# Attention over two head slots at a time in a one-layer decoder kernel

## What is computed

```
ada = silu(c) @ W_ada + b_ada              # shift1, scale1, gate1, shift2, scale2, gate2
u   = LN(x) * (1 + scale1) + shift1
xp, q, k, v, g_p, g_a = split(u @ w_in)    # 512 | 768 | 768 | 768 | 1024 | 1024
for group, (window, dilation) in enumerate(((128, 1), (512, 4), (2048, 16))):
    s = q_h @ k_h.T * 64 ** -0.5           # 4 heads of 64 a group; causal, windowed, dilated mask
    p = exp(s - max(s)); den = sum(p); o = p @ v_h / den; lse = max(s) + log(den)
attn   = sum over groups of softmax(lse over groups) * o      # one result a head slot
merged = sigmoid(g_p) * (pool_y @ w_pool_out) + sigmoid(g_a) * (attn @ w_attn_out)
x   = LN(alpha * x + (1 + gate1) * (merged @ w_o))
u2  = LN(x) * (1 + scale2) + shift2
x   = LN(alpha * x + (1 + gate2) * moe(u2))                   # top 4 of 32 clamped SwiGLU experts
```

## Time and profile before

| | us |
|---|---|
| median of 3 executions | 1194.89 (1194.87 to 1195.72) |
| the profiled execution, its own time | 1195.32 |
| its span in the profile | 1193.5 |
| PE busy | 1141.9 (96%) |
| DVE busy | 341.6 (29%) |
| ACT busy | 130.9 (11%) |
| DMA over the span | 461.84 MB, 387 GB/s |

### The profile page before, as it was taken

One profiled execution on the slowest core, in us unless ns is written; L12 is line 12 of the kernel. 1 busy time (PEld: TensorE's weight loads), 2 busy tenths in 40 slices (PEclk: granted clock), 3 DMA queues, 4 the chain that ended last, 5 costly groups with the idle time before them and its releaser, 6 DMA issues.

```text
span 1193.5 us, 13616 instructions
## 1 busy us (share of the span) xinstructions
PE 1141.9 (96%) x5749; PEld 558.1 (47%) x5749; DVE 341.6 (29%) x623; ACT 130.9 (11%) x228; POOL 17.0 (1%) x27
## 2 busy tenths in 40 slices
PE   4999999999999999999999999999999999999996
PEld 1768887554444444444444444444444434444342
DVE  4296563461112211222111211111111112222113
ACT  1212332021001000100000000000000000000001
POOL 0000400000000000000000000000000000000000
PEclk9999999999999999999999999999999999999999
DMA  9999639468899999999999999999999999999994
GB/s 369 356 326 344 220 146 382 181 276 357 343 429 427 427 427 428 428 427 429 429 427 427 429 429 428 427 429 430 429 426 429 429 429 428 427 429 429 428 417 197
DMA packets 55785, 461.84 MB, mean 387 GB/s; under 512 B 5694, under 2 KB 7742, under 8 KB 29770
## 3 DMA queue, kind: packets, MB, share of 16 engines
q1 hardware_dynamic: 52256, 458.24, 92.4%
q10 hardware_dynamic: 3498, 3.15, 0.9%
HBM read 460.33 MB, written 1.05 MB: 387 GB/s over the span
## 4 chain that ended last, share of the span: by engine, by line
PE 71%; DMA 26%; DVE 2%; ACT 0%; SPq 0%; issue 0%; DVEq 0%; ACTq 0%
PE bank L1347 38%; DMA ring<-w_up 23%; PE bank L1188 10%; PE bank L1333 7%; PE bank L1373 4%; PE bank L1278 2%; DMA ring<-w_in 2%; PE bank L1462 2%; PE bank L1264 2%; PE bank L1180 2%; PE bank L1367 1%; PE bank L1354 1%; PE bank L1212 1%; PE bank L1228 1%; PE bank L1339 0%; PE bank L1167 0%
## 5 line engine op out<-in xcount | busy, mean ns | idle before, releaser
L1347 PE MATMUL bank<-ring,feat_region 128*64 128x512 f32 x2944 | 649.1, 595 | 20.0 <-DMA ring<-w_up 19.3
L1347 PEld LDWEIGHTS bank<-ring,feat_region 128*64 128x64 f32 x2944 | 205.0, 137 | 439.0 <-issue 397.0
L1333 PEld LDWEIGHTS bank<-row_region,ln_tok 128*128 128x128 f32 x1024 | 116.7, 192 | 20.3 <-issue 19.4
L1333 PE MATMUL bank<-row_region,ln_tok 128*128 128x64 f32 x1024 | 121.1, 276 | 0.7 <-DVE row_region L927 0.7
L1188 PE MATMUL bank<-feat_region,ring 128*128 128x256 f32 x512 | 114.8, 385 | 2.8 <-DMA ring<-w_in 2.8
L1188 PEld LDWEIGHTS bank<-feat_region,ring 128*128 128x128 f32 x512 | 97.7, 192 | 20.7 <-issue 4.5
L984 DVE TENSOR_TENSOR gate_region<-bank,row_region 128x512 f32<-128x512 f32 x31 | 21.4, 692 | 249.3 <-PE bank L1347 249.3
L962 DVE TENSOR_SCALAR gate_region<-bank 128x512 f32<-128x512 f32 x31 | 21.4, 692 | 202.9 <-PE bank L1354 202.9
L974 DVE TENSOR_SCALAR acc_region<-bank 128x512 f32<-128x512 f32 x31 | 21.4, 692 | 178.0 <-PE bank L1354 178.0
L1373 PE MATMUL bank<-gate_region 64*128 64x512 f32 x264 | 65.8, 616 | 0.8 <-DVE gate_region L1007 0.8
L648 ACT ACTIVATE gate_region<-bank 128x256 f32<-128x256 f32 x31 | 11.9, 385 | 470.6 <-PE bank L1339 470.6
(11 more groups left out here) (220 smaller groups left out, 530.2 us busy)
## 6 DMA issues: line engine op xcount, KB each, us to landing
ring<-w_gate SPq DMA_DIRECT2D x62, 2048.0 KB, 28.0
ring<-w_down SPq DMA_DIRECT2D x62, 2048.0 KB, 33.3
ring<-w_up SPq DMA_DIRECT2D x60, 2048.0 KB, 31.9
ring<-w_in SPq DMA_DIRECT2D x9, 2048.0 KB, 13.0
ring<-w_ada SPq DMA_DIRECT2D x8, 2048.0 KB, 14.4
ring<-w_ada SPq DMA_DIRECT2D x8, 1024.0 KB, 15.4
ring<-w_o SPq DMA_DIRECT2D x2, 2048.0 KB, 10.0
ring<-w_gate SPq DMA_DIRECT2D x4, 1024.0 KB, 31.4
```

Of the source, the lines that this page charges most:

```text
L1333: last = nc.tensor.matmul(M_BANK[:, k * CAP:(k + 1) * CAP], u2[:, t, k * P:(k + 1) * P], pick_tok[:, b, t, :], start=t == 0, stop=t == NT - 1)
L1347: last = nc.tensor.matmul(dst[hf * CAP:(hf + 1) * CAP, :], lhs(k0 + k), tiles[k][:, hf * HALF:(hf + 1) * HALF], start=first and k == 0, st ...
```

## The change

Attention runs over two pairs a of head slots, 2a and 2a + 1. In a pair the two heads of a group lie on different row halves of the same `qk` tile, and their score products are issued in turn (hs = 0, hs = 1), each into a bank of its own. Two jobs follow, then the transposes of both slots, a third job, and the value products, also in turn between the two column halves of bank 3; behind them the fourth job. DVE does the softmax of both slots in one go, then two `ada` units. The four conditioning sums for rows 6 to 9 get a buffer of their own each (`late_acc`), so that `ada(6)` to `ada(9)` wait for nobody, and PE adds them up in one go, four products on four groups of 32 columns, behind the value products of the second pair. The second set of probabilities lies in `ln_tok` (the normalised input, which is no longer needed) and in the old cosine table. `row_max`, `row_sum` and `row_inv` get four columns each. The arithmetic is the same.

```diff
@@ -149,8 +149,9 @@
...
         v_tok = view(ring, late + 3072, NT * ATTN_WIDTH).rearrange("p (t n) -> p t n", t=NT)
-        probs = view(ring, late + 4608, 1152)
-        probs_t = view(ring, late + 5760, 1152).rearrange("p (g n) -> p g n", g=NG)
+        probs = [view(ring, late + 4608, 1152), view(ln_tok, 0, 1152)]
+        probs_t = [[view(ring, late + 5760 + 384 * g, 384) for g in range(NG)],
+                   [view(ln_tok, 1152, 384), view(ln_tok, 1536, 384), view(ring, late + 6912, 384)]]
@@ -170,6 +171,7 @@
...
         ada_acc = acc_region[:, :].rearrange("p (b n) -> p b n", b=2)
+        late_acc = view(row_region, D, 4 * HALF).rearrange("p (b n) -> p b n", b=4)
@@ -233,7 +235,9 @@
...
                 ctx.enter_context(nc.psum_tensor(f"bank{b}", [P, HALF], F32)) for b in range(8)]
-        T_BANKS = (4, 0, 1)
+        T_BANKS = ((0, 1, 2), (4, 5, 0))
+        LATE_SCORES = (bank[2], bank[4])
+        LAST_SCORES = (bank[5][:, 0:S], bank[3][:, S:2 * S])
@@ -428,7 +432,7 @@
...
                 else:
-                    sp.wait_ge(attn_done, 1)
+                    sp.wait_ge(attn_done, 2)
@@ -567,22 +571,28 @@
...
                 job(n)
-            for s in range(HEAD_SLOTS):
+            for a in range(HEAD_SLOTS // 2):
+                first = JOB_GATES + 4 * a
                 for t in range(NT):
-                    act.wait_ge(scores_read, 2 * s + t + 1)
-                    part = probs[:, 384 * t:384 * t + 384 * (t + 1)]
-                    nc.scalar.activation(part, part, ACT.Exp, bias=row_max[:, t:t + 1],
-                                         accum_out=row_sum[:, t:t + 1]).then_inc(exp_ready, 1)
-                job(JOB_GATES + 2 * s)
-                for g in range(NG):
-                    act.wait_ge(probs_t_done, NG * s + g + 1)
-                    nc.scalar.activation(probs_t[:, g, :], bank[T_BANKS[g]][:, 0:384], ACT.Copy) \
-                      .then_inc(probs_t_read, 1)
-                if s == HEAD_SLOTS - 1:
+                    for hs in range(2):
+                        act.wait_ge(scores_read, 4 * a + 2 * t + hs + 1)
+                        part = probs[hs][:, 384 * t:384 * t + 384 * (t + 1)]
+                        n = 2 * t + hs
+                        nc.scalar.activation(part, part, ACT.Exp, bias=row_max[:, n:n + 1],
+                                             accum_out=row_sum[:, n:n + 1]).then_inc(exp_ready, 1)
+                job(first)
+                job(first + 1)
+                for hs in range(2):
+                    for g in range(NG):
+                        act.wait_ge(probs_t_done, 6 * a + NG * hs + g + 1)
+                        nc.scalar.activation(probs_t[hs][g], bank[T_BANKS[hs][g]][:, 0:384], ACT.Copy) \
+                          .then_inc(probs_t_read, 1)
+                job(first + 2)
+                if a == 1:
...
                     nc.scalar.activation(ada2_rows, bank[5][:, :], ACT.Copy).then_inc(ada2_copied, 1)
-                job(JOB_GATES + 2 * s + 1)
-            act.wait_ge(attn_done, 1)
+                job(first + 3)
+            act.wait_ge(attn_done, 2)
@@ -762,10 +772,10 @@
...
             def ada(j):
-                if j >= 6:
-                    dve.wait_ge(acc_read, j - 5)
+                if j >= 10:
+                    dve.wait_ge(acc_read, j - 9)
                 landed(dve, ("ada", j))
-                w, acc = unit_view(("ada", j)), ada_acc[:, j % 2, :]
+                w, acc = unit_view(("ada", j)), late_acc[:, j - 6, :] if 6 <= j < 10 else ada_acc[:, j % 2, :]
@@ -830,32 +840,36 @@
...
             dve.wait_ge(ld_masks, 16)
-            for s in range(HEAD_SLOTS):
+            flat = masks.rearrange("p g k n -> p (g k n)")
+            for a in range(HEAD_SLOTS // 2):
                 for t in range(NT):
-                    dve.wait_ge(scores_done, 2 * s + t + 1)
...
+                    dve.wait_ge(scores_done, 4 * a + 2 * t + 2)
+                    for hs in range(2):
+                        part = probs[hs][:, 384 * t:384 * t + 384 * (t + 1)]
+                        if t == 0:
+                            step(nc.vector.scalar_tensor_tensor(
+                                out=part.rearrange("p (g n) -> p g n", g=NG),
+                                in0=bank[hs][:, 0:384].rearrange("p (g n) -> p g n", g=NG), scalar=HEAD_DIM ** -0.5,
+                                in1=masks[:, :, 1, :], op0=ALU.mult, op1=ALU.add))
+                        else:
+                            step(nc.vector.scalar_tensor_tensor(
+                                out=part[:, 0:512], in0=LATE_SCORES[hs][:, :], scalar=HEAD_DIM ** -0.5,
+                                in1=flat[:, 0:512], op0=ALU.mult, op1=ALU.add))
+                            step(nc.vector.scalar_tensor_tensor(
+                                out=part[:, 512:768], in0=LAST_SCORES[hs], scalar=HEAD_DIM ** -0.5,
+                                in1=flat[:, 512:768], op0=ALU.mult, op1=ALU.add))
+                        n = 2 * t + hs
+                        step(nc.vector.tensor_reduce(row_max[:, n:n + 1], part, AX.X, ALU.max, negate=True),
+                             scores_read)
                 for t in range(NT):
-                    part = probs[:, 384 * t:384 * t + 384 * (t + 1)]
-                    dve.wait_ge(exp_ready, 2 * s + t + 1)
-                    step(nc.vector.reciprocal(row_inv[:, t:t + 1], row_sum[:, t:t + 1]))
-                    step(nc.vector.tensor_scalar(part, part, row_inv[:, t:t + 1], None, ALU.mult), probs_ready)
-                ada(8 + s)
+                    for hs in range(2):
+                        part = probs[hs][:, 384 * t:384 * t + 384 * (t + 1)]
+                        n = 2 * t + hs
+                        dve.wait_ge(exp_ready, 4 * a + n + 1)
+                        step(nc.vector.reciprocal(row_inv[:, n:n + 1], row_sum[:, n:n + 1]))
+                        step(nc.vector.tensor_scalar(part, part, row_inv[:, n:n + 1], None, ALU.mult), probs_ready)
+                ada(8 + 2 * a)
+                ada(9 + 2 * a)
@@ -1159,13 +1173,11 @@
...
-            def row_group(j):
-                pe.wait_ge(acc_ready, j - 3)
-                if j == 6:
-                    pe.wait_ge(row_ready, 2)
-                rows = slice(32 * (j - 6), 32 * (j - 5))
-                nc.tensor.matmul(bank[5][rows, :], one.to_broadcast([P, 32]), ada_acc[:, j % 2, :],
-                                 start=True, stop=True).then_inc(acc_read, 1)
+            def row_groups():
+                pe.wait_ge(acc_ready, 6)
+                for g in range(4):
+                    nc.tensor.matmul(bank[5][32 * g:32 * g + 32, :], one.to_broadcast([P, 32]), late_acc[:, g, :],
+                                     start=True, stop=True).then_inc(acc_read, 1)
@@ -1197,43 +1209,53 @@
...
             job(10)
-            row_group(6)
             pe.wait_ge(rotated, QT)
-            for s in range(HEAD_SLOTS):
+            pe.wait_ge(row_ready, 2)
+            for a in range(HEAD_SLOTS // 2):
+                first = JOB_GATES + 4 * a
+                halves = [slice(HEAD_DIM * hs, HEAD_DIM * (hs + 1)) for hs in range(2)]
...
                     for g in range(NG):
-                        head = g * HEAD_SLOTS + s
-                        rows = slice(HEAD_DIM * (head % 2), HEAD_DIM * (head % 2 + 1))
-                        q = qk[rows, head // 2, t * P:(t + 1) * P]
-                        keys = qk[rows, QT + head // 2, 0:(t + 1) * P]
-                        dst = bank[0][:, g * P:(g + 1) * P] if t == 0 else \
-                            bank[1 + g // 2][:, (g % 2) * S:(g % 2 + 1) * S]
-                        last = nc.tensor.matmul(dst, q, keys, start=True, stop=True)
-                    last.then_inc(scores_done, 1)
-                job(JOB_GATES + 2 * s)
-                pe.wait_ge(probs_ready, 2 * (s + 1))
+                        tile = (g * HEAD_SLOTS + 2 * a) // 2
+                        for hs in range(2):
+                            if t == 0:
+                                dst = bank[hs][:, g * P:(g + 1) * P]
+                            else:
+                                dst = LATE_SCORES[hs][:, g * S:(g + 1) * S] if g < 2 else LAST_SCORES[hs]
+                            last = nc.tensor.matmul(dst, qk[halves[hs], tile, t * P:(t + 1) * P],
+                                                    qk[halves[hs], QT + tile, 0:(t + 1) * P], start=True, stop=True)
+                            if g == NG - 1:
+                                last.then_inc(scores_done, 1)
+                job(first)
+                job(first + 1)
+                for hs in range(2):
+                    pe.wait_ge(probs_ready, 4 * a + 3 + hs)
+                    for g in range(NG):
+                        if (hs, g) == (1, 2):
+                            pe.wait_ge(probs_t_read, 6 * a + 1)
+                        dst = bank[T_BANKS[hs][g]]
+                        nc.tensor.transpose(dst[:, 0:P], probs[hs][:, g * P:(g + 1) * P], ident)
```

(66 more changed lines are left out.)

## The result

| | before | changed |
|---|---|---|
| median of 4 executions each, us | 1195.31 (1194.87 to 1195.78) | 1185.90 (1182.98 to 1186.72) |
| ratio, 95% interval | | 0.9911 (0.9896 to 0.9927) |
| profiled execution, us | 1195.32 | 1185.53 |
| its span, mean granted clock | 1193.5, 0.996 | 1183.7, 0.993 |

The change is faster by 0.9%, 9.4 us in the medians. The forecast was 1183.2, in a range of 1182.2 to 1187.2. The four executions of the changed kernel spread over 3.7 us, where the forecast had counted on 0.85, and the fastest, 1182.98, has the highest mean clock of the four (0.995 against 0.993, 0.992, 0.992).

What follows compares the result with a forecast made beforehand. PE was taken to bound attention, with the gain carried through the transfer-bound expert tail. Scores 4.32, value products 4.32, sums 2.91 and transposes 0.10 give 11.65 us less: 1194.89 - 11.65 = 1183.2 us, range 1182.2 to 1187.2.

Steps and rivals of the forecast that it cites:

- Rival A: Attention's score and value products: halves share the array only partly, 8.25 us less, 1186.6 us; chance 0.14.
- the estimate from the Trainium skill: Attention's paired products: two tiles run 1.55 times as fast, kernel near 1186.0 us.
- no change: Attention's jobs on PE: eight before and after, taken to gain nothing.
- From there each event should stand 11 to 12 us earlier: After the last gates job: branch products, gather and first full DMA window all move 11 to 12 us earlier.
- At the full granted clock: Whole kernel before the change: PE busy in nearly every slice, at full clock; expected to stay at 1.00.
- The cover: DVE's softmax of a pair: ready 11.8 us after scores begin, PE asks after 16.4, 4.6 us of slack.
- Without the second job this would cost 2.5 us a pair: Between a pair's scores and transposes: with only one job, PE would wait 2.5 us a pair for probabilities.
- Rival D: Between the pairs: a late weight unit makes DVE the bound and the kernel slower, 1198 us; chance 0.03.
- The reading of the tail: Expert loop: the last 500 us are bound by transfers, but the stream starts and ends earlier when PE arrives earlier.
- rival C: Late expert stream: bound by transfers, its start doesn't move and absorbs the gain, 1194.9 us; chance 0.03.
- Rival B: Attention: short products on two halves run in sequence; only sums and transposes gain, 3.0 us, 1191.9 us; chance 0.04.
- over PE without a break: Attention before the change: the chain of waits is 82.30 us of PE work in sequence, 112.67 to 194.97.

Runs made afterwards that it cites:

- e1: Changed kernel with one extra 256-column product in each of PE's two routing-stage waits: 1181.94 us, ratio 0.9882.
- e4: Kernel before with one extra 256-column product in each of PE's two routing-stage waits: 1195.14 us, ratio 0.9988.
- e11: Kernel before without the two filler products after the second token tile's router products, which widens PE's wait ahead of the ranking: 1199.47 us, ratio 1.0022.
- e3: Changed kernel with two filler products, 1.55 us of PE, ahead of the first pair's scores: 1183.81 us, ratio 0.9892.
- e2: Changed kernel run again without edits, on the same chip as e1: 1185.00 us, ratio 0.9907.
- e8: Changed kernel with one job instead of two between a pair's scores and transposes, the other behind the value products: last job ends at 183.84 instead of 182.13.
- e9: e1 plus filler products in PE's front waits, two before the first conditioning rows' turn and six before the first job: 1181.91 us, ratio 0.9879.

## Why the prediction came out as it did

**The direction and the stage's mechanism held.** The terms of the sum, forecast and measured:

| less by, us | forecast | measured |
|---|---|---|
| scores, 8.64 to 4.34 | 4.32 | 4.30 |
| value products, 8.66 to 4.20 | 4.32 | 4.46 |
| conditioning sums, 3.88 to 0.99 | 2.91 | 2.89 |
| transposes, 4.20 to 3.92 | 0.10 | 0.28 |
| jobs, 56.88 to 56.04 | 0 | 0.84 |
| stage | 11.65 | 12.8 |

Rival A did not come: 2.17 us of scores a pair, not 2.78, and 2.10 of values, not 3.24. By the estimate from the Trainium skill, "TensorE: Matmul & The Clock Gate", section "Measured speedup vs the span model", a pair would have taken 2.79 us. This trace has 2 x 2.16 / 2.17 = 1.99 times for the row halves and 2.06 for the column halves, so here the estimate was too cautious.

**The term that was mis-sized is the jobs**, put at "no change". In the kernel before, each follows scores, value products or sums, which use half or a quarter of the array, and takes 7.10 or 7.12 us. In the change, two of a pair's four no longer do: one follows another job, one follows the transposes, which use the whole array like the jobs, and each of these takes 6.91 us: 14.01 + 6.91 + 7.10 = 28.02 us a pair, not 28.44.

**The step that failed is the one behind the stage**: "From there each event should stand 11 to 12 us earlier", with the clock at 1.00. The gather did, 12.86 us earlier; then the clock fell and took 3.1 us. The sum had no term for the clock. The kernel before showed no fall behind attention, and I read its 0.64 and 0.72 us waits as harmless; e1 shows that they are not, and e4 and e11 that the kernel before is exposed too. "At the full granted clock" was also wrong as it stands: the window from 30 to 60 had 0.94. The Trainium skill's "TensorE: Matmul & The Clock Gate", in its section "Part 1: The HAM clock gate", says that the gate's phase isn't set by the kernel's start, so one kernel meets it differently from run to run. The spread of e3, 7.7 us over six executions of one kernel, fits that; no trace here shows the phase itself.

**That the median fell into the range is partly luck.** It missed the forecast by 2.7 us: 1.2 better in the stage, 3.1 lost at the clock, and 0.8 because the profiled execution lies 0.4 under its median here, where the forecast counted on 0.4 over. 1185.90 lies in the part of the range that was put there for rival A, which did not happen. And the 11.4 us of e2 come near 11.65 only because a larger gain and the clock's loss nearly cancel; with the fillers in both kernels the gain is 13.2.

**The cover was read too strictly.** The two softmaxes took 9.7 us (113.64 to 123.32), not 10.84. "Without the second job this would cost 2.5 us a pair" came out at 0.8 in e8: PE's first transposes need the even slot's probabilities alone, and these are ready 9.9 us after the pair's start, while the sum let PE wait for both slots at 11.8. Rival D is out with 7.30 us of idle DVE. ada(8) ended 5.0 us later than before, not "some 3", and nothing waited for it.

**The reading of the tail was right** (rival C out): 12.88 us gained at the second gather of e1 are 13.2 in its span, and 9.74 in the changed kernel are 9.8. Rival B is out by the 24 records in 2.17 us. One detail of the head was not: "over PE without a break" leaves out that the chain of the kernel before passes through ACT's copies for 1.0 us in each slot, ahead of the value products. In the change a job stands there, and the chain stays on PE.

The version that beats both is e1, 1181.94 us, 1.2% under the kernel before; e9 equals it.

## What to carry to other kernels

Small products on separate row or column halves cost here the time of one set if they take turns product by product; grouping them by half gave away 0.5 and 1.35 us a pair. When a stage ahead of a short wait of PE is shortened or lengthened, look for such waits behind it and fill them in both kernels, with products whose result nobody uses, before judging the change: two fillers of 0.44 us each raised the measured gain from 11.4 to 13.2 us and took most of the spread out of the changed kernel's times (not out of the kernel before, 3.0 us with them). One profiled execution at full clock does not show that a wait is safe: three here went through at 1.00, four with the same waits did not.

## What was not expected of the hardware

Waits of 0.63 and 0.72 us, 0.24 us of work apart, were enough for a fall to half clock in some executions, with PE busy all through the windows before and after (245 to 248, 251 to 260). Products issued half by half still overlapped: 2.70 us for 24 score records, where six of 128 and six of 256 columns a half, one after another, would take about twice the 2.16 of one slot. And the multiply-adds of the first conditioning unit took 9.49 us, against 6.26 for each of the three units after it. Beside the first ran POOL's large operations (L1115, 248 to 1020 columns, 125.23 to 133.94); beside the second POOL was at work too, but on 16 and 240 columns. That points to the large ones; no run isolates it, and it cost nothing here only because DVE had room.
